# The entrance of attention: four units' scores ahead of the last query product, other PSUM banks, and an earlier reset of the score banks

## What is computed

```python
qa, ka, va, qb, kb, vb, iq, ik, iw, ga, gb = split_projection(rmsnorm(xp, g_attn[i]), w_in[i])
s = einsum('bnqkgd,bnskd->bnkgqs', qg, k) * ATTN_SCALE
s = where(valid, s + bias, -inf)
m = maximum(max(s), sk)                       # sk: the head's sink
e = exp(s - m)
pr = e / (sum(e) + exp(sk - m))
o = einsum('bnkgqs,bnskd->bnqkgd', pr, v)
# branch B: top 128 keys by an indexer's score, then the same softmax without a sink
x = x + (sigmoid(ga) * (oa @ w_branch_a) + sigmoid(gb) * (ob @ w_branch_b)) @ w_out
```

## Time and profile before

| | |
|---|---|
| median of 3 runs | 1036.11 us (1035.64 to 1037.59) |
| profiled execution | 1036.8 us |
| its span | 1035.0 us |
| TensorE busy | 925.9 us (89%) |
| VectorE busy | 378.2 us (37%) |
| ScalarE busy | 256.5 us (25%) |
| GpSimd busy | 132.4 us (13%) |
| chain that ended last | PE 63%, DMA 29%, DVE 4%, ACT 2% |

### The profile page before, as it was taken

The page is one execution under the profiler, slowest core; times in us unless marked ns, Lnnn a source line. Parts: engine busy times, 40 slices in busy tenths (PEclk is TensorE's granted clock), DMA queues, the critical chain, the costliest instruction groups (busy, mean ns, idle before and its releaser), DMA issues.

```text
span 1035.0 us, 14155 instructions
## 1 busy us (share of the span) xinstructions
PE 925.9 (89%) x5699; PEld 591.2 (57%) x5702; DVE 378.2 (37%) x974; ACT 256.5 (25%) x523; POOL 132.4 (13%) x136
## 2 busy tenths in 40 slices
PE   7989999999999999998999977877887888887996
PEld 7869995456999998994333322322322222234775
DVE  4179996764233436453111101101101011102796
ACT  6244326764323233221000000000000000001542
POOL 2403701113030000001111110011010110000000
PEclk9999998999999999997999999999999899999998
DMA  9850602002834316366999999999999999996601
GB/s 265 118 152 2 203 1 62 1 2 68 263 105 120 78 46 244 128 236 239 427 427 425 427 428 428 424 428 425 429 426 426 427 426 425 427 428 264 254 22 66
DMA packets 60132, 263.72 MB, mean 255 GB/s; under 512 B 11054, under 2 KB 36030, under 8 KB 46224
## 3 DMA queue, kind: packets, MB, share of 16 engines
q1 hardware_dynamic: 54160, 250.99, 63.0%
q0 software_dynamic: 5296, 9.79, 2.6%
q10 hardware_dynamic: 624, 2.23, 0.6%
HBM read 253.99 MB, written 16.85 MB: 262 GB/s over the span
## 4 chain that ended last, share of the span: by engine, by line
PE 63%; DMA 29%; DVE 4%; ACT 2%; issue 1%; SPq 1%; DVEq 0%; ACTq 0%
DMA arena<-in_w_up 25%; PE ps L1111 13%; PE ps L1278 12%; PE ps L980 5%; PE ps L1143 4%; PE ps L1426 4%; PE ps L1303 3%; PE ps L881 3%; PE ps L952 3%; DMA arena<-in_w_ple 2%; PE ps L1044 2%; PE ps L1014 2%; PE ps L1065 2%; PE ps L1399 1%; PE ps L1172 1%
## 5 line engine op out<-in xcount | busy, mean ns | idle before, releaser
L1278 PE MATMUL ps<-arena,hT 128*64 128x512 f32 x960 | 234.5, 641 | 39.4 <-DMA arena<-in_w_up 39.2
L1278 PEld LDWEIGHTS ps<-arena,hT 128*64 128x64 f32 x960 | 71.6, 141 | 199.3 <-issue 149.4
L2211 DVE TENSOR_TENSOR xf<-xf,ps 128x256 f32<-128x256 f32 x32 | 13.5, 421 | 401.6 <-ACT xf L1699 379.1
L1111 PE MATMUL ps<-arena_merge,arena_merge 128*128 128x256 f32 x624 | 99.7, 287 | 0.0
L1303 PE MATMUL ps<-arena,xf 128*64 128x512 f32 x336 | 76.7, 598 | 12.8 <-DVE xf L2214 12.8
L1111 PEld LDWEIGHTS ps<-arena_merge,arena_merge 128*128 128x128 f32 x624 | 87.4, 188 | 0.0
L836 POOL DMA_INDIRECT expert_rows<-xf,arena x32 | 32.2, 1007 | 425.6 <-ACT xf L1703 399.8
L1111 PE MATMUL ps<-xf_merge,arena_merge 128*128 128x256 f32 x480 | 82.0, 288 | 0.0
L1699 ACT ACTIVATE xf<-ps 128x256 f32<-128x256 f32 x30 | 11.6, 385 | 259.1 <-PE ps L1278 259.1
L1111 PEld LDWEIGHTS ps<-xf_merge,arena_merge 128*128 128x128 f32 x480 | 69.3, 188 | 0.0
L1703 ACT ACTIVATE xf<-ps 128x512 f32<-128x512 f32 x30 | 17.9, 598 | 159.8 <-PE ps L1303 159.8
(11 more groups left out here) (309 smaller groups left out, 1311.1 us busy)
## 6 DMA issues: line engine op xcount, KB each, us to landing
arena<-in_w_gate SPq DMA_DIRECT2D x30, 2048.0 KB, 29.4
arena<-in_w_up SPq DMA_DIRECT2D x30, 2048.0 KB, 37.0
arena<-in_w_down SPq DMA_DIRECT2D x11, 2048.0 KB, 36.4
hT<-in_w_down SPq DMA_DIRECT2D x11, 2048.0 KB, 36.5
arena<-in_w_down SPq DMA_DIRECT2D x20, 1024.0 KB, 32.2
arena<-in_w_in SPq DMA_DIRECT2D x10, 1024.0 KB, 6.2
arena<-in_w_in SPq DMA_DIRECT2D x3, 2048.0 KB, 10.5
arena<-in_w_gate SPq DMA_DIRECT2D x8, 512.0 KB, 9.0
```

The source lines that it names most:

```text
L1111: mm = pe.matmul(w[:, 2 * lo_t:lo_t + hi_t], rounded(st[:, c, cols]), rounded(mv[:, c, lo_t:hi_t]), start=c == 0 and k == 0, stop=c == pla ...
L1278: mm = pe.matmul(ps[g * BLK:(g + 1) * BLK, 2 + s, :], xsT[:, c, col:col + BLK], expert_columns(k, slice(0, 2), c, g), start=c == 0, stop=c ...
```

## The change

Six edits go together:
- `qa` is projected by m = 0, 2, 1, 3 (`QA_ORDER`), so the heads of units 0 to 3 come first. The splitting of the weights follows this order.
- TensorE scores units 0 and 1 and units 2 and 3 (block 0) before the last product, m = 3. That product goes to banks 6 and 7 and not to its ring slot. Behind it come the turns of units 0 and 1, then the scores of units 4 and 5, which wait for its copy.
- Scores are in banks 2 to 5, turned weights in banks 0 and 1 (before: 0 to 3 and 4 to 5).
- ScalarE does exponentials 0 and 1 before it copies the last product out.
- VectorE zeroes the columns of the score banks after five of the sample's ten rounds, for which it waits for the copy of the second product.
- GpSimd sets masks and sinks in the bias tiles, chained one after the other, before it splits the weights of `qa`. It waits there for the tables' transfers (`toep_moved`) and the constants.

```diff
-    + [(('qb', m), 'act') for m in range(4)] + [(('qa', m), 'act') for m in range(4)], 3)
+    + [(('qb', m), 'act') for m in range(4)] + [(('qa', m), 'act') for m in QA_ORDER], 3)
...
-        return ps[:, first:first + 2, :].rearrange("p b n -> p (b n)") if first < 3 else ps[:, 3, :]
+        return ps[:, first + 2:first + 4, :].rearrange("p b n -> p (b n)") if first < 3 else ps[:, 5, :]
...
@@ GpSimd
+        pool.wait_ge(toep_moved, 16 + 16 * 10)
+        pool.wait_ge(consts_in, 16 * CONSTS)
+        link(pool.memset(toep_a[0:CHUNK, :, TW - CHUNK:TW], -BIG))
+        link(pool.memset(toep_a[CHUNK:P, :, 0:CHUNK], -BIG))
+        link(pool.tensor_scalar(toep_a[:, :, TW:TW + 1], sink_in[:, :].unsqueeze(2), -1.0, None, ALU.mult))
+        for hh in range(HG):
+            link(pool.tensor_scalar(toep_sa[32 * hh:32 * hh + NS, :, WIN + NS:WIN + NS + 1],
+                                    sink_in[32 * hh:32 * hh + NS, hh:HEADS:HG].unsqueeze(2), -1.0, None, ALU.mult))
+        pool.sem_inc(toep_ready, 1)
+
+        query_weights_low(7, slab[1], qx, QA_ORDER)
...
@@ TensorE
+        for m in range(4):
+            project_queries('qb', m, m)
+        for n, m in enumerate(QA_ORDER[:-1]):
+            project_queries('qa', m, 4 + n)
+
+        pe.wait_ge(wide_out['dve'], WIDE_DONE['dve'])
+        pe.wait_ge(wide_out['act'], WIDE[('qa', QA_ORDER[1])].out)
         for by in ('dve', 'act'):
-            pe.wait_ge(wide_out[by], WIDE_DONE[by])
             pe.wait_ge(narrow_out[by], NARROW_DONE[by])
...
             if u == 0:
-                pe.wait_ge(toep_ready, 1)
+                pe.wait_ge(toep_ready, 2)
...
-            w = ps[:, 4:6, :].rearrange("p b n -> p (b n)")
+            w = ps[:, 0:2, :].rearrange("p b n -> p (b n)")
...
         scores_of_two(0)
         for u in range(len(UNITS) + WEIGH):
+            if u == 1:
+                project_queries('qa', QA_ORDER[-1], 7)
+                pe.wait_ge(wide_out['act'], WIDE[('qa', QA_ORDER[2])].out)
+                turn(0)
+                turn(1)
+            if u == 2:
+                pe.wait_ge(wide_out['act'], WIDE_DONE['act'])
             if u % 2 == 0 and u + AHEAD < len(UNITS):
                 scores_of_two(u + AHEAD)
-            if LAG <= u < len(UNITS) + LAG:
+            if LAG + 2 <= u < len(UNITS) + LAG:
                 turn(u - LAG)
...
@@ ScalarE
+            if u == 2:
+                queries_out('qa', QA_ORDER[-1])
             act.wait_ge(max_ready, u + 1)
...
@@ VectorE
-            for _ in range(SELECT_FIRST if b == 's' else TOPK_P // 8):
+            for k in range(SELECT_FIRST if b == 's' else TOPK_P // 8):
+                if b == 's' and k == SELECT_FIRST - SELECT_LATER:
+                    dve.wait_ge(wide_out['act'], WIDE[('qa', QA_ORDER[1])].out)
+                    dve.memset(ps[:, 2:6, P:P + 1], 0.0)
+                    dve.memset(ps[:, 2:6, 2 * P:2 * P + 1], 0.0).then_inc(toep_ready, 1)
                 next_eight(b)
                 take_eight(b)
...
-        dve.wait_ge(toep_moved, 16 + 16 * 10)
-        dve.memset(toep_a[0:CHUNK, :, TW - CHUNK:TW], -BIG)
-        dve.memset(toep_a[CHUNK:P, :, 0:CHUNK], -BIG)
-        dve.tensor_scalar(toep_a[:, :, TW:TW + 1], sink_in[:, :].unsqueeze(2), -1.0, None, ALU.mult)
...
-        dve.wait_ge(wide_out['act'], WIDE_DONE['act'])
-        dve.memset(ps[:, 0:4, P:P + 1], 0.0)
-        dve.memset(ps[:, 0:4, 2 * P:2 * P + 1], 0.0).then_inc(toep_ready, 1)
...
+        dve.wait_ge(toep_ready, 2)
         row_max(0)
```

More of the change, by code:

```diff
@@ L137 @@
 BLOCKS = [1, 2, 3, 's']
+QA_ORDER = [0, 2, 1, 3]
 WIDE, WIDE_DONE = ring(
@@ L165 @@
 UNITS_A = len(UNITS) // 2
-SELECT_FIRST = 10
+SELECT_FIRST, SELECT_LATER = 10, 5
 SELECT_AT = [9, 17, 25, UNITS_A + 1, UNITS_A + 4, UNITS_A + 7, UNITS_A + 10]
@@ L761, in _, with query_weights_low @@
         low(slab_kva, kv_hi['a'], "front").then_inc(sw_split, 1)
-        def query_weights_low(first, s, dst):
-            for m in range(4):
-                pool.wait_ge(sw_high, first + m)
+        def query_weights_low(first, s, dst, order):
+            for m in order:
+                pool.wait_ge(sw_high, first + order.index(m))
                 low(s[:, 0:4, m * P:(m + 1) * P], q_hi(dst, m, 0), "front")
                 low(s[:, 4:8, m * P:(m + 1) * P], q_hi(dst, m, 1), "front").then_inc(sw_split, 1)
-        query_weights_low(3, slab[0], qb)
+        query_weights_low(3, slab[0], qb, [0, 1, 2, 3])
         pool.wait_ge(narrow_out['act'], NARROW[('kvb', 4)].out)
@@ L970, in _, with project_queries @@
             pe.transpose(w[:, past:past + NS], kv_n[0:NS, 4, 0:P], ident[0:NS, 0:NS]).then_inc(wide_full, 1)
[L972 to L983, removed]
+        def project_queries(q, m, nth):
+            s, dst = (slab[0], qb) if q == 'qb' else (slab[1], qx)
+            w = wide(open_slot(WIDE, (q, m), wide_out) if (q, m) != ('qa', QA_ORDER[-1]) else 3)
+            pe.wait_ge(sw_split, 3 + nth)
+            for c in range(KD):
+                hi, lo = q_hi(dst, m, c // 4)[:, c % 4, :], s[:, c, m * P:(m + 1) * P]
+                for k, (st, mv) in enumerate(((hi, hT_f), (hi, hT_lo), (lo, hT_f))):
+                    for a in range(2):
+                        mm = pe.matmul(w[:, a * 512:a * 512 + HALF], rounded(st, "front"),
+                                       rounded(mv[:, c, a * HALF:(a + 1) * HALF]), start=c == 0 and k == 0,
+                                       stop=c == KD - 1 and k == 2)
+            mm.then_inc(wide_full, 1)
+        for m in range(4):
[4 more added lines that the diff above has]
+        pe.wait_ge(wide_out['act'], WIDE[('qa', QA_ORDER[1])].out)
         for by in ('dve', 'act'):
-            pe.wait_ge(wide_out[by], WIDE_DONE[by])
             pe.wait_ge(narrow_out[by], NARROW_DONE[by])
@@ L1507, in _, with query_weights_high @@
             act.activation(rounded(ik_hi[:, lo:lo + cols], "front"), w[:, 0:cols], ACT.Copy).then_inc(ik_high, 1)
-        def query_weights_high(s, dst):
-            for m in range(4):
+        def query_weights_high(s, dst, order):
+            for m in order:
                 high(q_hi(dst, m, 0), s[:, 0:4, m * P:(m + 1) * P], "front")
```

35 lines of the change are left out of this document (18 added, 17 removed).

## The result

Five runs of each kernel gave 1029.85 us for the changed one (1029.55 to 1031.94) and 1035.64 us for the one before (1034.63 to 1037.59): a ratio of 0.9946 (0.9933 to 0.9959). In these runs it is 5.8 us faster, where 3.9 were forecast, and 1029.85 lies under the forecast range of 1031.0 to 1036.2.

The account below looks back on a forecast made before the run. The prediction took the chain of waits at the projection-attention seam, and perhaps the slow clock behind it, as the cost. 1036.8 - 1.3 (seam) - 2.6 (clock) - 0.69 (to the median) gave 1032.2 us, range 1031.0 to 1036.2.

Parts of the forecast that it names:

- The seam: From last query product to unit 8's scores: these come 1.31 us earlier, bounds 0.5 to 1.6.
- Rival 2: At the seam, early scores bring nothing, ScalarE stays the limit, product's delay eats the gain: 1035.4 to 1036.1 us; chance 0.11.
- VectorE's seven operations: Two memsets and five small operations leave VectorE's queue; hidden under the last product before, they give nothing by themselves.
- the sum: Whole kernel: 1036.8 less 1.3 for the seam, 2.6 for the clock and 0.69 to the median, 1032.2 us.
- GpSimd: Bias setup before splitting the last query weights takes 2.1 us, leaves 3.2 us of room and costs nothing.
- Rival 3: GpSimd's setup past 5.3 us makes TensorE wait for the first split; 1038.5 us at 9 us; chance 0.09 with companion.
- The clock: Behind the seam the clock more likely holds; block 1 takes about 8.45 for 11.06 us, 2.6 us gained.
- The same shapes: Block 2 has block 1's shapes plus one 1 us ScalarE splitting operation, so its 8.45 us prices block 1.
- The upper bound of 3.3: Most the clock term could gain in block 1, where ScalarE's 6.90 us of work in 10.16 becomes the limit.
- More often than to fall: Behind the last product the clock was expected to hold more often than fall, TensorE busy some 3.7 us.
- Rival 1: The clock falls behind the seam all the same, leaving only the 1.3 us gain: 1034.8 us; chance 0.30.
- Transfers: SyncE's first gate chunk starts 0.7 us later, is done by 168.8, and stays hidden with 1.6 us of room.

Follow-up runs that it names:

- experiment 5: The changed kernel run again unaltered; 1031.78 us in 12 runs, ratio 0.9971.
- experiment 1: The kernel before, with six extra 128x128 products filling TensorE's idle stretch behind the last query product; 1032.33 us in 5 runs, ratio 0.9964.
- experiment 9: The changed kernel with units 0 to 3's scores behind the last product, its copy ahead of all exponentials, five extra products in TensorE's idle stretch; 1031.24 us.
- experiment 3: The changed kernel with the bias tiles' masks and sinks set by VectorE again, ahead of its first row maximum; 1034.27 us in 11 runs, ratio 0.9992.
- experiment 4: The changed kernel with ScalarE copying the last query product out ahead of exponentials 0 and 1; 1033.84 us in 12 runs, ratio 0.9981.

## Why the prediction was wrong

**The seam: right in size, its source in part another.** Forecast 1.31 us for unit 8's scores, measured 1.21 in the profiled pair and again in experiment 5 (52.25, the same place); 0.10 of it is the clock, since the kernel before with its clock held (experiment 1) has 53.36. Most places came within 0.3 us once the 0.94 us of the start are taken off: scores ahead at 154.37 (forecast 154.5), product's end 161.3 (161.2), scores behind it 162.65 (162.65), unit 8 at 164.17 (164.07). Rival 2, early scores that bring nothing, doesn't hold as it was put. But its half sentence that scores without exponentials are worthless is close to it: experiment 9 has all four exponentials behind the copy and all scores behind the product, and is 0.06 us later. So the 1.1 us come neither from the scores nor from the exponentials ahead, which pay just for the product's delay; they come from what no longer stands between the copy and the first exponential, namely the reset, the scores behind it and their row maxima, for which ScalarE waited 1.18 us. Which of the earlier reset, the order of the products and the other banks this needs isn't shown, since all experiments on the changed kernel keep the three.

**VectorE's seven operations: wrong, without effect on the sum.** "They hid under the last product before and give nothing by themselves" was true of the old order. In the new one exponentials 0 and 1 must be over before the product ends, and by experiment 3 the seven operations, set back, cost 1.1 us (1.3 with the lower clock), all of the seam gain. The sum was right, since it took the row maxima at the end of the rounds, that is, with the operations gone; but in this order the gain hangs on them as much as on the reset.

**GpSimd: the result right, the room wrong.** The setup took 2.83 us from 129.18 to the first split at 132.01, not 2.1: 0.26 and 0.28 us for a tiny operation where 0.15 was taken, 0.52 for a memset where 0.46 was. It also started later; in the time of before 130.1, not 128.5. The first pair is split at 134.5, and TensorE, whose first `qa` product stands at some 135.4 (the forecast's 136.34 less 0.94), doesn't wait: its products follow one another without a gap from 133 to 138. Of the 3.2 us of room some 0.9 are left. Rival 3 didn't occur, and it was nearer than its 0.09 suggests.

**The clock: the cause right, the size wrong. This is the step that failed.** The forecast said that "block 1 takes about what block 2 took, 8.45 for 11.06: 2.6 us more". It took 7.13, so the term is 3.93. The prediction itself wrote that block 2 has one splitting operation of ScalarE more (1.05 us), and didn't take it off. And block 1 has less for TensorE as well, since what it turns and weighs beside its own scores is still in part block 0, with 128 keys: before and after, its timeline has 11 records of turns and 8 of products with the values in block 1, and 16 and 16 in block 2. The first rows are of block 1 in the changed kernel, the last of block 2:

```profile
165.22 0.65 PE L1082 MATMUL ps<-hT,x_nat 128*64 128x256 f32 x4
...
168.55 0.65 PE L1082 MATMUL ps<-hT,x_nat 128*64 128x256 f32 x4
...
172.58 1.08 PE L1082 MATMUL ps<-hT,x_nat 128*64 128x256 f32 x8
```

"The same shapes" held for the scores alone. The upper bound of 3.3 failed too: it set ScalarE's 6.90 us against the 10.16 us of the slow clock, where block 1 is 11.06 long. Taken over the whole block, from one score to the next, the profile of before has the rows that were needed:

```profile
165.38:176.44 11.06, 11.06 (x41) 4.74 (x40) 5.67 (x21) 7.21 (x28) 1.75 (x3) 0.55 0.23 53
176.44:184.89 8.45, 8.25 (x53) 4.08 (x53) 6.22 (x24) 8.22 (x26) 2.08 (x3) 1.00 0.01 3
```

ScalarE's 7.21 us bound the term at 11.06 - 7.21 = 3.85. That this is so near to 3.93 is in part luck, for ScalarE isn't what sets block 1's length. At the whole clock TensorE is busy 6.83 and ScalarE 6.91 of the 7.13 us (experiment 1), and the chain of the changed kernel goes over TensorE and VectorE from 163.0 to 171.4, without ScalarE, for instance:

```profile
167.55 0.70 PE ps L1031 x4
...
168.62 0.58 PE ps L1082 x4
169.20 0.86 PE ps L1093 x4
```

TensorE's records of block 1, priced by their distances in block 2 of the kernel before (scores 0.158 us, turns 0.19, products with the values 0.12, the spreading of the sums 0.24), come to an estimate of 6.5 us, so the rows of before allowed a term between 2.6 and 4.5.

With 3.93 instead of 2.6 the sum is 1030.9 us; the 12 lower runs of the changed kernel have a median of 1031.15. The first five runs lie another 1.1 us under that sum; the profiled pair differs outside the entrance as well, by 0.94 us ahead of it and 1.0 behind block 1, which is no part of the change.

The reason given for the clock to hold was mis-sized too. In the 4.64 us behind the product TensorE was to be busy 3.7; it was busy 2.94, against 2.23 before, and it idled 1.12 us and not 0.9 ahead of its scores. "More often than to fall" came true, in 12 of 17 runs, on a narrower footing than was thought.

**Rival 1: it is there.** It was put as one of two futures, at 0.30, with 1034.8 us. It is a share of the executions: 5 of 17 lie at 1033.67 to 1035.85 with a median of 1033.82. By the means, the change is 1.2 us always, and 3.9 us times the rise of the share that keeps its clock, from 9 to 14 of 83 to 12 of 17: 1.2 + 3.9 x (0.71 - 0.11 to 0.17) = 3.3 to 3.5, where the means differ by 3.49. The forecast was made as if one execution stood for all. Over all 17 runs the median, 1031.62, is inside the range that the first five missed; this is no merit of the sum, whose term for block 1 stays 1.3 us too small.

On the Trainium skill's page TensorE: Matmul & The Clock Gate, section "A second HAM failure mode: psum-queue depth-cycling", short gaps between groups of matmuls make the clock go back and forth (seen there in another kernel, with bf16 products of 512 columns), and the prediction weighed this as a reason for the fall to stay. At the seam the runs bear it out in part: in the profiled executions every gap of 1.36 us or more was followed by a fall, and two of 0.9 close together as well, while one of 0.91, one of 1.11 and one of 1.12 were not. It doesn't hold inside the blocks: the groups of blocks 1 and 2, with gaps of 0.31 and 0.20 us, kept the whole clock whenever the seam did, and blocks 2 and 3 had it even in the kernel before.

**Transfers: right.** SyncE's gate chunk was through by 168, ScalarE's first splitting began at 168.97 and didn't wait. What was won stayed: blocks 2 and 3, and the windows near 250 and 390, are all 6.08 us earlier.

**Open.** Why the same kernel keeps its clock in one execution and loses it in another, and why the times of experiments 3 and 4 spread over 8 to 9 us, isn't settled. The share of before's runs that keep it (9 to 14 of 83) is uncertain, since other slow stretches, near 15, 64 and 470 in its profiled execution, move a run by a microsecond or so.

## What to carry to other kernels

A TensorE idle stretch can cost more behind it than in itself: here one of 1.58 us was followed by 3.9 us more in block 1. Ask what it costs if the clock falls. Where its length couldn't be cut, four to six small products into unread PSUM columns took the fall away here at no cost. Price a slow stretch at the whole clock by its own work, counted record by record, and let the other engines' busy time in that same stretch bound it; don't take a later one that looks alike, for work that lags by some units makes the first block a different one. And where the times of one kernel lie in two groups, a handful of runs can show just one: count the runs in each before a difference is explained.

## What the runs showed of the hardware that was not expected

- In one and the same order of work the length of one idle stretch goes with how often the clock falls, not just whether: 10 of 10 runs in the lower group at 0.23 us, 12 of 17 at 1.12, at most 2 of 12 at 2.27.
- Once down, the clock stayed at the lower level for some 10 us (165.1 to 175.3) though TensorE was busy in all of them; that, not the gap, is the price.
- On GpSimd a `tensor_scalar` of 128 by 8 elements took 0.26 us and four of 32 by 2 in a chain took 1.11 together, and a memset of 64 by 512 took 0.52; on VectorE the memset took 0.48 and four of the small ones 0.68 together.
